# Mixer C's scores of two head pairs as four products of high and low parts, with the first weights' low parts and the last tile's output rearranged

## The reference

```python
qc  = apply_rope(qc.reshape(B, T, G, h, 64)...)      # 6 query heads, scaled
ksl = apply_rope(_to_kv(ksl, B, T), ...)             # keys, selected branch
kwi = apply_rope(_to_kv(kwi, B, T), ...)             # keys, window branch
...
# with SEQ = 512 every block is selected and the window covers all: two causal softmaxes
p_slc = masked_softmax(einsum('bghqd,bgqkd->bghqk', qb, ks) * scale, smask)
p_win = masked_softmax(einsum('bghqd,bgkd->bghqk', qb, kw) * scale, wmask)
o     = stack([o_cmp, o_slc, o_win], -1)             # mixed by three sigmoid gates
...
mix = einsum('btm,md->btd', concatenate([o_a, o_b, o_c], -1), w_out[l])
x = layer_norm(ALPHA * x + mix, ln1_g[l], ln1_b[l])
hid = square(relu(einsum('btd,df->btf', x, w_up[l])))
x = layer_norm(ALPHA * x + einsum('btf,fd->btd', hid, w_down[l]), ln2_g[l], ln2_b[l])
```

## Time and profile before

| | |
|---|---|
| median of 3 runs | 1260.64 us |
| the profiled execution | 1260.26 us, of which its span 1258.4 us |
| PE busy | 1237.9 us (98%), 7118 matmuls |
| DVE busy | 725.6 us (58%) |
| ACT busy | 477.6 us (38%) |
| POOL busy | 493.0 us (39%) |
| attention tasks of mixer C, layer 0 and 1 | about 168 to 231 us and 788 to 851 us of the span |

### The profile page before, as it was taken

One profiled execution on the slowest core, in us unless ns is written; L12 is line 12 of the kernel. 1 busy time (PEld: TensorE's weight loads), 2 busy tenths in 40 slices (PEclk: granted clock), 3 DMA queues, 4 the chain that ended last, 5 costly groups with the idle time before them and its releaser, 6 DMA issues.

```text
span 1258.4 us, 17853 instructions
## 1 busy us (share of the span) xinstructions
PE 1237.9 (98%) x7118; PEld 1028.7 (82%) x7118; DVE 725.6 (58%) x1117; ACT 477.6 (38%) x946; POOL 493.0 (39%) x279
## 2 busy tenths in 40 slices
PE   7999999999999999999999999999999999999997
PEld 7998766789888888888899976668988888888885
DVE  4395778369672262360397868783796623605406
ACT  5226688523232221222143366784333322222210
POOL 3468000134544444444345760003264444444442
PEclk9999999999999999999999999999999999999999
DMA  7433001123523332233224320013233332332211
GB/s 252 124 80 102 2 18 35 67 84 102 162 94 101 101 99 88 98 101 96 63 60 128 93 68 1 18 52 100 69 129 105 101 100 89 97 101 101 96 55 67
DMA packets 77826, 110.04 MB, mean 87 GB/s; under 512 B 17648, under 2 KB 38448, under 8 KB 77616
## 3 DMA queue, kind: packets, MB, share of 16 engines
q1 hardware_dynamic: 76160, 104.11, 27.4%
q10 hardware_dynamic: 1584, 4.78, 1.2%
HBM read 106.78 MB, written 2.10 MB: 87 GB/s over the span
## 4 chain that ended last, share of the span: by engine, by line
PE 91%; DVE 4%; issue 1%; ACT 1%; POOL 1%; DMA 0%; DVEq 0%; POOLq 0%; ACTq 0%
PE ps L678 16%; PE ps L679 16%; PE ps L680 16%; PE ps L675 9%; PE ps L674 9%; PE ps L676 9%; PE ps L781 3%; PE ps L769 3%; PE ps L818 2%; PE ps L803 1%; PE ps L633 1%; DVE negmax L1390 1%; ACT probs_a L1134 1%; PE ps L894 1%; PE ps L856 1%
## 5 line engine op out<-in xcount | busy, mean ns | idle before, releaser
L542 POOL TENSOR_TENSOR w_lo<-raw,w_hi 128x1024 fp32r<-128x1024 f32 (+3 forms) x184 | 425.0, 2314 | 644.7 <-ACT w_hi L1006 644.2
L1006 ACT ACTIVATE w_hi<-raw 128x1024 fp32r<-128x1024 f32 (+3 forms) x200 | 199.0, 996 | 598.2 <-PE ps L680 365.7
L674 PE MATMUL ps<-xt_hi,w_lo 128*128 128x512 f32 (+1 forms) x576 | 210.7, 366 | 0.0
L675 PE MATMUL ps<-xt_hi,w_hi 128*128 128x512 f32 (+1 forms) x576 | 210.5, 365 | 0.0
L676 PE MATMUL ps<-xt_lo,w_hi 128*128 128x512 f32 (+1 forms) x576 | 210.5, 365 | 0.0
L678 PE MATMUL ps<-w_hi,xt_lo 128*128 128x384 f32 (+3 forms) x448 | 152.0, 339 | 1.6 <-DVE xt_lo L1242 1.1
L678 PE MATMUL ps<-w_hi,mt_lo 128*128 128x512 f32 x384 | 150.1, 391 | 0.0
L679 PE MATMUL ps<-w_hi,mt_hi 128*128 128x512 f32 x384 | 149.4, 389 | 0.0
L680 PE MATMUL ps<-w_lo,mt_hi 128*128 128x512 f32 x384 | 149.4, 389 | 0.0
L680 PE MATMUL ps<-w_lo,xt_hi 128*128 128x384 f32 (+3 forms) x448 | 147.5, 329 | 0.0
L679 PE MATMUL ps<-w_hi,xt_hi 128*128 128x384 f32 (+3 forms) x448 | 147.4, 329 | 0.0
(11 more groups left out here) (175 smaller groups left out, 1875.1 us busy)
## 6 DMA issues: line engine op xcount, KB each, us to landing
raw<-in_w_up SPq DMA_DIRECT2D x64, 512.0 KB, 3.7
raw<-in_w_down SPq DMA_DIRECT2D x64, 512.0 KB, 3.9
raw<-in_w_in SPq DMA_DIRECT2D x32, 384.0 KB, 3.3
raw<-in_w_in SPq DMA_DIRECT2D x16, 256.0 KB, 2.8
raw<-in_w_in SPq DMA_DIRECT2D x32, 128.0 KB, 2.9
raw<-in_w_out SPq DMA_DIRECT2D x8, 512.0 KB, 3.4
raw<-in_w_out SPq DMA_DIRECT2D x12, 256.0 KB, 3.7
rows<-in_ln_g ACTq DMA_DIRECT2D x4, 512.0 KB, 4.3
```

Source lines behind the costliest of these rows:

```text
L542: nc.gpsimd.tensor_tensor(unit_of(w_lo, u), unit_of(raw, u), unit_of(w_hi, u).bitcast(F32), ALU.subtract).then_inc(s_lo_ready, 1)
L674: mm(o, wl[:, c], a_hi[:, k, cols], start=first, stop=False)
L675: mm(o, wh[:, c], a_hi[:, k, cols], start=False, stop=False)
L1006: A(unit_of(w_hi, u), unit_of(raw, u), ACT.Copy).then_inc(s_hi_ready, 1)
```

## The change

Three edits are made together.

1. The scores of mixer C's second and third pair (tasks 23 to 32) are made of all four products of high and low parts of queries and keys, instead of one fp32 product. The parts are made by four new POOL instructions (two copies, two subtractions, each 128 x 1024), after the last input unit has been used and `ks` has been copied; PE waits for them (`c_split`) before task 23. `qc_lo` takes the place of `qc`'s second and third part.
2. At the start of layer 0 the low parts of units 0 and 1 are made on DVE, before slice 0 and between slices 1 and 2, and no longer on POOL.
3. At the end tile 2 is scaled and stored before tile 3, and tile 3 is scaled and stored in two halves of 512 columns.

```diff
+        qc_hi, qc_lo = at("qc_hi", ra + 20480, [2, SEQ], F32R), at("qc_lo", rc + 2048, [2, SEQ], F32R)
+        ks_hi, ks_lo = at("ks_hi", ra + 24576, [2, SEQ], F32R), at("ks_lo", ra + 28672, [2, SEQ], F32R)
...
-            for n, tt in enumerate((0, 1, 3, 2)):
-                sp.wait_ge(s_out_last, n + 1)
+            for tt in range(3):
+                sp.wait_ge(s_out_last, tt + 1)
                 sp.dma_start(out[0, tt * P:(tt + 1) * P, :], xres[:, tt]).then_inc(s_stored, 16)
-            sp.wait_ge(s_stored, 16 * TT)
+            for half in range(2):
+                sp.wait_ge(s_out_last, 4 + half)
+                c = slice(512 * half, 512 * half + 512)
+                sp.dma_start(out[0, 3 * P:4 * P, c], xres[:, 3, c]).then_inc(s_stored, 16)
+            sp.wait_ge(s_stored, 16 * (TT + 1))
...
             for layer in range(DEPTH):
-                if layer == 0:
-                    split(layer, 0, 2)
                 split(layer, 4, U_LAST - 2)
...
+                pool.wait_ge(s_unit_used, nth("unit_used", layer, U_OUT))
+                pool.wait_ge(s_side_emptied, nth("side_emptied", layer, SIDE_END[14]))
+                nc.gpsimd.tensor_copy(ks_hi[:], ks[:])
+                link(nc.gpsimd.tensor_copy(qc_hi[:], qc[:, 1:3]))
+                nc.gpsimd.tensor_tensor(ks_lo[:], ks[:], ks_hi[:].bitcast(F32), ALU.subtract)
+                nc.gpsimd.tensor_tensor(qc_lo[:], qc[:, 1:3], qc_hi[:].bitcast(F32), ALU.subtract).then_inc(s_c_split, 1)
...
+                if t >= TASKS_A + PAIR_C:
+                    if t == TASKS_A + PAIR_C:
+                        pe.wait_ge(s_c_split, nth("c_split", layer, 1))
+                    terms = [(q, k, pair - 1) for q in (qc_lo, qc_hi) for k in (ks_lo, ks_hi)]
+                else:
+                    terms = [(qc, ks, pair)]
...
+                    for queries, keys, p in terms:
+                        for hh, o in enumerate(banks):
+                            r = 64 * hh
+                            last = mm(o[:, 0:2 * n]..., queries[r:r + 64, p, i * P:n], keys[r:r + 64, 0:2, 0:n], ...)
+                elif t >= TASKS_A:
+                    for _, i, m, n, at_ in tiles:
+                        for queries, keys, p in terms:
+                            for hh, o in enumerate(banks):
+                                r = 64 * hh
+                                last = mm(o[:, at_:at_ + n], queries[r:r + 64, p, i * P:n], keys[r:r + 64, m, 0:n], ...)
...
+                def scale_and_shift(tt, parts=1):
...
+                    n = D // parts
+                    for c in range(0, D, n):
+                        xs = xres[:, tt, c:c + n]
+                        V.scalar_tensor_tensor(xs, xs, rstd[:, tt:tt + 1], rows[:, 1, c:c + n], ALU.mult, ALU.add).then_inc(s_out_last, 1)
...
-                        if tt in (0, 1, 3):
+                        if tt < 2:
                             scale_and_shift(tt)
                     scale_and_shift(2)
+                    scale_and_shift(3, 2)
...
                 if layer == 0:
-                    split_x(layer, 0, 0, range(5))
+                    low_unit(layer, 0)
+                    split_x(layer, 0, 0, (0, 1))
+                    low_unit(layer, 1)
+                    split_x(layer, 0, 0, (2, 3, 4))
                     low_unit(layer, 2)
```

More of the change, by code:

```diff
@@ L193 @@
     oa_squared=3, rms_ready=3, oa_normed=3, oa_hi=3, oa_mixed=3,
-    oc_hi=3, oc_mixed=3,
+    c_split=1, oc_hi=3, oc_mixed=3,
     stats=2 * TT, rstd=2 * TT, rows=64, rows_used=1, hid_hi=32, hid_ready=32, mlp_evac=4 * N_MLP,
@@ L373, in build @@
         s_oa_squared = sem("oa_squared")
+        s_c_split = sem("c_split")
         s_rms_ready = sem("rms_ready")
@@ L752, in scores @@
                     masks(o, tiles)
+                if t >= TASKS_A + PAIR_C:
[4 more added lines that the diff above has]
+                    terms = [(qc, ks, pair)]
                 if both_maps(t):
                     _, i, _, n, _ = tiles[0]
[L756 to L759, removed]
+                    for queries, keys, p in terms:
+                        for hh, o in enumerate(banks):
+                            r = 64 * hh
+                            last = mm(o[:, 0:2 * n].rearrange("p (m n) -> p m n", m=2), queries[r:r + 64, p, i * P:n], keys[r:r + 64, 0:2, 0:n],
+                                      start=False, stop=keys is ks or (queries is qc_hi and keys is ks_hi), skip_group_check=True)
+                elif t >= TASKS_A:
[3 more added lines that the diff above has]
+                                r = 64 * hh
+                                last = mm(o[:, at_:at_ + n], queries[r:r + 64, p, i * P:n], keys[r:r + 64, m, 0:n],
+                                          start=False, stop=keys is ks or (queries is qc_hi and keys is ks_hi), skip_group_check=True)
                 else:
@@ L762, in scores @@
                         for hh, o in enumerate(banks):
[L763 to L768, removed]
+                            r = 32 * (2 * hh + m)
+                            queries, keys = qa[pair][r:r + 32, i * P:n], ka[r:r + 32, pair, 0:n]
                             last = mm(o[:, at_:at_ + n], queries, keys, start=False, stop=True, skip_group_check=True)
@@ L1247, in low_unit @@
                 g = layer * UNITS + u
-                dve.wait_ge(s_lo_ready, nth("lo_ready", layer, u))
+                if g:
+                    dve.wait_ge(s_lo_ready, nth("lo_ready", layer, u))
                 dve.wait_ge(s_hi_ready, nth("hi_ready", layer, u + 1))
@@ L1288, in sums_of @@
                     V.tensor_scalar(mv[:, tt, 1:2], mv[:, tt, 1:2], LN_EPS, None, ALU.add).then_inc(s_stats, 1)
-                def scale_and_shift(tt):
+                def scale_and_shift(tt, parts=1):
                     dve.wait_ge(s_rstd, nth("rstd", layer, TT + tt + 1))
                     dve.wait_ge(s_out_centred, tt + 1)
-                    V.scalar_tensor_tensor(xres[:, tt], xres[:, tt], rstd[:, tt:tt + 1], rows[:, 1], ALU.mult, ALU.add) \
-                        .then_inc(s_out_last, 1)
+                    n = D // parts
+                    for c in range(0, D, n):
+                        xs = xres[:, tt, c:c + n]
+                        V.scalar_tensor_tensor(xs, xs, rstd[:, tt:tt + 1], rows[:, 1, c:c + n], ALU.mult, ALU.add).then_inc(s_out_last, 1)
                 if final:
```

## The result

| | median | runs | ratio to before, 95% interval |
|---|---|---|---|
| before | 1260.55 us | 7 | |
| after | 1264.60 us | 7 | 1.0032 [1.0023, 1.0041] |

The change makes the kernel 4.05 us slower. The forecast was 1267.0 us, its own range 1263.5 to 1270, the range for 8 in 10 1260.5 to 1276; the measured time lies in both.

A forecast was written before the change was run, and what follows sets the result against it. PE was taken to bound the kernel (91% of the chain). Products +2.8, stall +5.4, start -1.4 and end -0.45 sum to +6.35, predicting 1267.0 us; own range 1263.5 to 1270, 8 in 10 1260.5 to 1276.

The forecast's parts named there:

- products: Scores of tasks 23 to 32: four fp32r products cost PE more than one fp32 product, +2.8 us in all.
- stall behind POOL: POOL's new operations hold DVE, so PE waits for task 17's probabilities: 2.7 us counted per layer, +5.4 in all.
- start: Layer 0's start: with both subtractions on DVE, slice 4's last product starts at 14.7 instead of 16.14, -1.4 us.
- end: Kernel's end: tile 2 scaled in the gap, tile 3's halves end 0.3 to 0.4 earlier, last transfer half as large, -0.45 us.
- Rival B: 128-column fp32r products take four cycles a column, 0.226 us instead of 0.107: 3.8 us more, 1270.8; chance 0.12.
- rival C: The two heads' fp32r score products don't overlap on PE: 22.7 us instead of 2.8, 1286.9; chance 0.10.
- the copy's price: Each 128x1024 copy on POOL taken as 1.6 us, between 1.2 (memset's rate) and 2.4 (the subtraction's).
- POOL's pauses: POOL and DVE take turns with exclusive use, so POOL's 8.1 us of work from 165.9 ends near 176.
- rows 6 and 7: Profile rows before: DVE's SBUF operations wait for POOL, a subtraction 2229 ns against 692, a tiny product 1.33 us against 0.16.
- PE begins at about 9.1: Start of layer 0: PE's first products begin at about 9.1, with slices 0 and 1 done by 11.5.
- A (DVE not held): POOL's operations fall between DVE's: 1258.8 with products free, chance 0.09; 1261.6 with the products' 2.8, chance 0.13.
- D (the clock falls after PE's stall): PE at half speed for as long as the stall: about 2.8 us more per layer at most, 1269 to 1272; chance 0.05.

The follow-up runs named there:

- copies_only: Kernel after with POOL's two copies but not its two subtractions, all four products taking the high parts: 1261.89 us, 1.47 more than before.
- start_end: Kernel before with the edits of the start and of the end, scores as before: 1259.21 us, 1.10 less than before.
- spread_warm: Kernel after with POOL's subtractions held back and 12 dummy products at the start: 1261.02 us, 0.63 more than before.
- start_end_warm: Kernel before with start and end edits and 12 dummy bf16 products before PE's first transpose: 1258.31 us, 2.00 less than before.
- pool_only: Kernel before with POOL's four new instructions and PE's wait for them, parts unused, scores still fp32: 1262.95 us, 2.53 more than before.
- start_only: Kernel before with the edit of the start alone: 1259.66 us, 0.76 less than before.
- end_only: Kernel before with the edit of the end alone: 1260.02 us, 0.40 less than before.
- heads_apart: Kernel after with all four products of head 0 queued before all four of head 1: 1265.28 us (4 runs), 4.89 more than before.
- spread: Kernel after with POOL's two subtractions held back until task 17's and task 18's probabilities are ready: 1261.40 us, 1.09 more than before.
- before_warm: Kernel before with only the 12 dummy products added ahead of PE's first transpose: 1260.36 us, 0.05 more than before.

## Why the prediction was right, and where it was off

| term | forecast | measured | by |
|---|---|---|---|
| products | +2.8 | +2.6 | `copies_only` less `start_end` (2.57), `spread_warm` less `start_end_warm` (2.63) |
| stall behind POOL | +5.4 | +2.5 | `pool_only` |
| start | -1.4 | -0.76 | `start_only` |
| end | -0.45 | -0.40 | `end_only` |
| sum | +6.35 | +3.9 | measured as a whole: +4.05 |

The sum came out 2.3 us too high, and it would have been further off had two terms not erred against each other: the stall was put 2.9 too high and the start's gain 0.6 too high. The lower end of the forecast's own range doesn't follow from the terms given beside it: with a stall of 1.8 a layer and products at nothing they give 1262.4, not 1263.5.

**The products.** Right in size and in its parts. A 128-column fp32r product takes what its weight load takes (0.11 us, forecast 0.107), so four cost about 0.17 more than fp32 by PE's rows and 0.21 by the medians (forecast 0.22); a task of 384 + 128 costs 0.23 more in all (forecast 0.27), one of 512 0.06 (forecast 0.05). 8 and 12 such tasks make 2.6. Rival B (0.226 each) and rival C (heads one after the other) are refuted by the rows of L784 and L777. The reason that I gave for the overlap, that the loop alternates the heads, is not needed (`heads_apart`).

**The stall.** The mechanism was right and its place too: PE before L803 of task 17, for probabilities that DVE finished late behind POOL. The size was off: 2.8 us per layer in the forecast (2.7 as counted), 1.41 of wait in PE's rows and 2.53 for both layers by `pool_only`. Two steps of the lay-out failed. The first is the copy's price. I took 1.6 us; the rows show 1.24 and 1.04, below even my lower end of 1.2 for the second. The other is POOL's pauses. I had put 8.1 us of work between 165.9 and near 176, so POOL was to stand for some 2 us while DVE had its turns. In the rows the four instructions follow each other without a pause, 165.66 to 172.88, which is the sum of their lengths (7.22), and the subtractions are hardly longer (2.41 and 2.53) than in `spread` (2.36 and 2.37): it was DVE that was held. The second subtraction then met DVE's maxima from PSUM and the tiny `facs`, not L1443, whose two halves I had put behind it. My lower bound of 1.8 per layer was too high for the same reason: with copies of 1.2 and no pauses my own prices, by estimate, let POOL end at 173.2 and L1443 at 174.6, 1.3 behind the 173.28.

Nor does the whole wait stay. From the start of the scores just ahead of task 17's transposes to these PE needs 2.55 us (171.85 to 174.40) instead of 1.06 (172.22 to 173.28), 1.49 more. From there to the transposes of task 18 it needs 2.74 (to 177.14) instead of 2.92 (to 176.20), since there PE had to wait for DVE before as well. That leaves 1.31 per layer, 2.6 in all. The forecast had counted on getting back 0.1 of 2.8.

The Trainium skill ("GPSIMD Engine Reference", Elementwise — side-by-side cycle accounting) has the rate from which the prediction made about 0.9 us for a copy; the trace shows 1.24 and 1.04, nearer to that than the 1.6 that I took from the memset's row. Its "SBUF — State Buffer" (SBUF: two separate sides) says that PE, ACT and the port pair that DVE has to itself never wait for another engine; the trace agrees: the maxima from PSUM take 1.27 us beside L612, and 1.29 with POOL idle. The prediction took this for granted of the maxima, and its rows 6 and 7 did not show it.

**The start.** DVE's chain came as laid out. Two steps failed. "PE begins at about 9.1" left out that PE's own transposes last until 9.86, 16 of them 0.213 apart; in the kernel before, too, the first product starts only at 9.93. And the "some slack, should its clock still be low there" was not enough: five products at 0.32 instead of 0.175 take about 0.75 us. `start_end_warm` shows both: with a raised rate the transposes are 0.11 apart and the products 0.175 from the first on, and ahead of slice 4's last product PE waits once for DVE. Even so PE's first product starts at 9.42 and not at 9.1, since x's second part arrives only for 8.46; the forecast had no term for that arrival. Start and dummy products together are worth 2.00 - 0.40 = 1.60 us by the medians, and 1.13 in the profiled execution (16.14 to 15.01), in which x arrives late (6.63). That the lower rate is what took most of the gain is shown by that pair of runs and `before_warm`; what makes the moments of the rate and of x's arrival vary from run to run is not.

**The end.** Right, 0.40, which is what DVE's last operation gained in the rows (0.39); nothing is seen of the smaller last transfer.

**The rivals.** A (DVE not held) is refuted by L1474's 3.28 us and by `pool_only`. D (the clock falls after PE's stall) did not come: PE's rows of L803 have the same 1.09 us behind the stall as before it.

**What stays open.** `spread` gained 2.96 against after by the medians, where the stall is worth 2.53. In the profiled executions it gained 2.92, of which 0.29 lie in the start (slice 4's last product at 15.49 instead of 15.78), so 2.6 are left for the stall. The runs of the kernels with the new start but without dummy products scatter over 1.2 to 1.7 us within a kernel, so medians of 4 to 11 runs don't settle differences of a few tenths.

## What to carry to other kernels

Here work on an idle GpSimd was not free while DVE worked on SBUF: lay such work over DVE's idle time and over its reads from PSUM. Two waits did that here and took the stall away. When an edit removes a gap of PE, ask what the gap was hiding; here it hid slow transposes and slow first products, and a few dummy products while PE waits for its first data gained 0.90 us where the edit alone had gained 0.76. When an fp32 product is split into four fp32r ones, the short tiles are the dear ones: about 0.17 us more for each of 128 columns, against 0.06 for a task of 512.

## What the runs showed of the hardware that I had not expected

**The clock column does not show the first rise.** In the busy times by stretch of the kernel after (columns as in the earlier trace rows) it reads 1.00 where products come at half rate:

```profile
10.50:11.00 0.50, 0.50 (x4) 0.50 (x3) 0.50 (x2) 0.50 (x2) 0.00 (x0) 1.00 1.04 416
```

The distance between starts does (0.32 us for 384 columns).

**A raised rate can be lost again in the waits of the start.** In the profile of `before_warm` PE runs the dummy products, the transposes and six products with waits between them, the last two of 0.88 and 0.81 us, and then has the lower level from 12.07 on, by the length of its products in the timeline (0.69 where it is 0.41 at the higher level, the first fence) and, this time, by the clock column of the busy times by stretch (the second, 0.51 for 12.0 to 15.4):

```profile
12.07 0.69 PE L683 MATMUL ps<-w_hi,xt_lo 128*128 128x384 f32 x1 [0.81 <-DVE xt_lo L1247]
```

```profile
12.00:15.40 3.40, 3.33 (x10) 3.33 (x11) 3.26 (x10) 2.32 (x4) 0.00 (x0) 0.51 1.05 424
```

This execution took 1261.80 us, another of the eleven 1262.30, the other nine 1260.02 to 1260.50.

**Two row halves of PE run ahead of each other.** In `heads_apart` each of head 1's first four products stands behind all four of head 0 in the queue, and yet starts only 13 to 17 ns after its counterpart of head 0.
